# Seven block products for the first two up blocks of each MLP chunk, and quadrant moves on ScalarE

## The reference, cut to what matters

```python
for layer in range(2):
    h = rmsnorm(x, norm_mix_w[layer])
    x = x + (hybrid_mixer(h, ...) if layer == 0 else swa_sink_attention(h, ...))
    h = rmsnorm(x, norm_mlp_w[layer])
    u = relu(h @ w_up[layer])             # w_up 2048 x 8192
    x = x + (u * u) @ w_down[layer]       # w_down 8192 x 2048
return rmsnorm(x, final_norm_w)
```

## Time and profile before

| | |
|---|---|
| median of three runs | 1994.04 us |
| the profiled execution | 1995.09 us |
| its span, first to last instruction | 1993.3 us |
| mean granted TensorE clock | 0.999 |
| PE busy | 1984.1 us, 100% |
| DVE busy | 1581.1 us, 79% |
| ACT busy | 1066.0 us, 53% |
| matmuls | 9089 |

### The profile page before, as it was taken

How to read it: one execution, slowest core, us unless ns; L and a number is a source line. 1 busy time by engine, 2 the same in 40 slices (tenths; PEclk the granted TensorE clock), 3 DMA queues, 4 the chain that set the end, 5 groups by cost and what they waited for, 6 DMA issues and landing times.

```text
span 1993.3 us, 25055 instructions
## 1 busy us (share of the span) xinstructions
PE 1984.1 (100%) x9089; PEld 1638.8 (82%) x9089; DVE 1581.1 (79%) x2190; ACT 1066.0 (53%) x1402; POOL 45.1 (2%) x55
## 2 busy tenths in 40 slices
PE   9999999999999999999999999999999999999998
PEld 7888888888888888888888878888888888888887
DVE  6777678989769868976889887989858876985875
ACT  6665665555445545544545566555445544544554
POOL 1110110000000000000000000000000000000000
PEclk9999999999999999999999999999999999999999
DMA  8556545655665475556655545564575555466563
GB/s 306 177 182 205 181 165 203 202 172 192 217 199 170 168 249 182 184 206 190 211 190 186 174 154 165 182 197 152 197 247 191 188 206 189 148 218 226 187 205 112
DMA packets 191758, 382.50 MB, mean 192 GB/s; under 512 B 6328, under 2 KB 7616, under 8 KB 191552
## 3 DMA queue, kind: packets, MB, share of 16 engines
q1 hardware_dynamic: 190288, 377.51, 56.5%
q0 software_dynamic: 1216, 3.88, 0.6%
q10 hardware_dynamic: 176, 0.07, 0.0%
HBM read 379.34 MB, written 2.10 MB: 191 GB/s over the span
## 4 chain that ended last, share of the span: by engine, by line
PE 98%; DVE 1%; issue 0%; ACT 0%; DMA 0%; ACTq 0%
PE acc L1399 26%; PE acc L1400 26%; PE acc L1401 26%; PE bank L1399 3%; PE bank L1400 3%; PE bank L1401 3%; PE acc L1426 1%; PE acc L1425 1%; PE acc L1427 1%; DVE area L1219 1%; PE bank L1427 1%; PE bank L1425 1%; PE bank L1426 1%; PE bank L1515 0%; PE bank L1592 0%; PE bank L1616 0%
## 5 line engine op out<-in xcount | busy, mean ns | idle before, releaser
L976 DVE TENSOR_TENSOR w_lo<-raw,w_hi 128x1024 fp32r<-128x1024 f32 x744 | 899.8, 1223 | 354.4 <-ACT w_hi L733 350.1
L733 ACT ACTIVATE w_hi<-raw 128x1024 fp32r<-128x1024 f32 x744 | 777.2, 1059 | 716.7 <-PE acc L1401 562.4
L1399 PE MATMUL acc<-w_hi,a_hi 128*128 128x512 f32 x1552 | 607.1, 391 | 0.0
L1401 PE MATMUL acc<-w_hi,a_lo 128*128 128x512 f32 x1552 | 604.1, 389 | 0.0
L1400 PE MATMUL acc<-w_lo,a_hi 128*128 128x512 f32 x1552 | 604.0, 389 | 0.0
L1399 PEld LDWEIGHTS acc<-w_hi,a_hi 128*128 128x128 f32 x1552 | 291.5, 188 | 61.2 <-issue 0.9
L1401 PEld LDWEIGHTS acc<-w_hi,a_lo 128*128 128x128 f32 x1552 | 291.4, 188 | 60.8
L1400 PEld LDWEIGHTS acc<-w_lo,a_hi 128*128 128x128 f32 x1552 | 291.4, 188 | 59.9
L1399 PE MATMUL acc<-w_hi,b_hi 128*128 128x512 f32 x784 | 305.7, 390 | 0.0
L1400 PE MATMUL acc<-w_lo,b_hi 128*128 128x512 f32 x784 | 305.3, 389 | 0.0
L1401 PE MATMUL acc<-w_hi,b_lo 128*128 128x512 f32 x784 | 305.0, 389 | 0.0
(11 more groups left out here) (240 smaller groups left out, 1296.8 us busy)
## 6 DMA issues: line engine op xcount, KB each, us to landing
raw<-in_mlp_w_up SPq DMA_DIRECT2D x128, 1024.0 KB, 5.4
raw<-in_mlp_w_down SPq DMA_DIRECT2D x128, 1024.0 KB, 5.1
raw<-in_hyb_w_in SPq DMA_DIRECT2D x44, 1024.0 KB, 5.3
raw<-in_attn_w_qkv SPq DMA_DIRECT2D x20, 1024.0 KB, 5.1
raw<-in_hyb_w_out SPq DMA_DIRECT2D x16, 1024.0 KB, 5.2
raw<-in_attn_w_out SPq DMA_DIRECT2D x16, 1024.0 KB, 5.1
raw<-in_hyb_w_in SPq DMA_DIRECT2D x5, 512.0 KB, 9.6
out_y<-x SPq DMA_DIRECT2D x4, 512.0 KB, 3.0
```

The lines of the kernel that those rows point to most:

```text
L733: nc.scalar.activation(w_hi[:, ring(b, h)], raw[:, q, 2 * e:2 * e + 2, :], ACT.Copy).then_inc(hi_ready, 2 if what == ("R", HALVES - 1) else 1)
L976: nc.vector.tensor_tensor(w_lo[:, ring(b, h)], raw[:, q, 2 * e:2 * e + 2, :], w_hi[:, ring(b, h)].bitcast(F32), ALU.subtract).then_inc(lo_ ...
L1399: nc.tensor.matmul(a, xh, wh, start=first, stop=False, skip_group_check=joins)
L1401: ins = nc.tensor.matmul(a, xl, wh, start=False, stop=last, skip_group_check=joins)
```

## The change

- The up blocks 0 and 1 of every chunk (8 pairs, `UP0`, `UP1`) become pairs with seven block products. Their steps are those of the down pairs up to R3, then L6, L7, a slot border, R4 to R7. They are no longer woven.
- The partial results are copied to tiles of their own, `part_l` and `part_r` (`add_part`), and `sum_pair` adds the accumulators to them; ACT takes relu from there.
- The token sums for the up pairs are made once for each MLP (`add_up_tokens` on DVE, in the slot of res 2, step 6), and cast for each chunk (`up_tokens` on ACT, `up_tokens_rest` on DVE: in the slot of res 3, steps 1 and 2, and in the later chunks in the second down pair, steps 12 and 13).
- For all up blocks and the last residual block ahead of each MLP, ACT moves the result into a tile `shifted` by 16 activations of 32 partitions x 256 elements, the square included (`squares`, `move_res`), at steps of their own. DVE then needs four transposes of 128 partitions x 256 elements (`turn_shifted`).
- The last residual block's x additions stay on DVE, one step later. Its sums of squares, root and inverse go from steps 1 to 5 to steps 10 to 13 of the up pair, and TensorE waits for its low parts ahead of L6.

```diff
-QUADRANTS_PAIR = {6: 4, 7: 4, 8: 4, 9: 4}
+SQUARES_UP0 = {2: 3, 3: 3, 4: 3, 5: 4, 6: 3}
+SQUARES_UP1 = {4: 4, 5: 4, 6: 4, 7: 4}
+SQUARES_AT = {0: 4, 1: 6, 2: 6}
+SQUARES_PAIR = {3: 2, 4: 2, 5: 2, 6: 2, 7: 2, 8: 2, 9: 2, 10: 2}
+RES_AT = {2: 1, 3: 3, 4: 1, 5: 1, 6: 1, 7: 4, 8: 1, 9: 4}
+LAST_SUMS_AT = 10
...
+UP0 = {m + PERIOD * c for m in (MLP0, MLP1) for c in range(CHUNKS)}
+UP1 = {b + 1 for b in UP0}
...
+MIXED = [("P", 1), ("L", 2), ("P", 5), ("L", 3), ("P", 2), ("P", 6), ("P", 4), ("L", 4), ("P", 7),
+         ("L", 5), ("P", 3), ("R", 2), ("R", 3)]
+DOWN_STEPS = MIXED + [("R", 4), ("R", 5), ("R", 6), ("R", 7), (None, 0), ("L", 6), ("L", 7)]
+UP_STEPS = MIXED + [("L", 6), ("L", 7), (None, 0), ("R", 4), ("R", 5), ("R", 6), ("R", 7)]
...
+            def squares(slot, k):
...
+                for n in range(done, done + at[k]):
+                    a, f = divmod(n, QUADRANTS)
+                    ins = nc.scalar.activation(shifted[f * QUAD:(f + 1) * QUAD, a], src[a * QUAD:(a + 1) * QUAD, :, :, f, :],
+                                               ACT.Square)
...
+                        if b in UP0:
+                            ins = nc.vector.tensor_copy((part_l, part_r)[side][:, tt, :], accumulator(right, src))
...
+            def sum_pair(slot, b):
+
+                part = up_stage(b)
+                dve.wait_ge(part_added, slot.pairs(4, 4, pair_of(b)[0]))
+                for tt in range(TT):
+                    nc.vector.tensor_tensor(part[:, tt, :], part[:, tt, :], accumulator(b, tt),
+                                            ALU.add).then_inc(pair_summed, 1)
...
+            def add_up_tokens(slot):
+
+                whole = part_l.rearrange("p t n -> p (t n)").rearrange("p (k s) -> p k s", k=4)
+                dve.wait_ge(turned_out, slot.count(N_TURNED, -1, INIT_HALVES))
+                link(nc.vector.tensor_tensor(whole, a_hi[:, 0:4, :].bitcast(F32), a_lo[:, 0:4, :].bitcast(F32), ALU.add))
...
+                link(nc.vector.tensor_tensor(s1, a21, a22, ALU.add))
+                nc.vector.tensor_tensor(s3, a11, a21, ALU.subtract)
+                link(nc.vector.tensor_tensor(s2, s1, a11, ALU.subtract))
+                nc.vector.tensor_tensor(s4, a12, s2, ALU.subtract).then_inc(up_added, 1)
...
+            def turn_shifted(slot, k, kind):
...
+                dst = turn.rearrange("p m (k t a c) -> p t (m k) a c", k=2, t=TT, a=QUADRANTS)
+                for a in range(QUADRANTS):
+                    ins = nc.vector.transpose(dst[:, :, :, a, :], shifted[:, a])
+                ins.then_inc(turned, 2)
...
+                    if (b in FIRST_PAIRS and what == ("R", 6)) or (b in (MLP0, MLP1) and what == ("L", 6)):
                         pe.wait_ge(turned_out, slot.count(N_TURNED, 0, INIT_HALVES))
```

More of the change, by code:

```diff
@@ L91 @@
 DIRECT = {"xb", "kv", "aq"}
-BY_QUADRANT = {"up", "res"} | DIRECT
+BY_QUADRANT = {"res"} | DIRECT
+BY_VECTOR = BY_QUADRANT | {"up"}
 SPLIT = {"g", "up", "res"}
@@ L125, with pair_of, unit_free, side_block @@
 SUM_COUNT = {5: 1, 7: 2, 6: 3, 4: 4}
-LAST_TURNED_AT = STEP_OF["R", 6]
+def pair_of(b):
+    first = b if b in PAIRS0 else b - 1
+    steps, units = (UP_STEPS, UP_UNITS) if first in UP0 else (DOWN_STEPS, DOWN_UNITS)
+    return first, steps, steps.index((None, 0)), units
+def unit_free(b, n):
+    _, steps, _, units = pair_of(b)
+    if n < 2:
+        return STEP_OF["P", 4 if n == 0 else 3] + 1
+    side, g = units[n]
+    return steps.index((side, 2 * g + 1)) + 1
+def side_block(b, side):
+    first = pair_of(b)[0]
+    return first + (side == ("R" if first in UP0 else "L"))
+LEFT = {side_block(b, "L"): (b in DOWN0 and b not in FIRST_PAIRS) for b in PAIRS0}
 WOVEN = ({MIX_OUT0, QKV0, ATT_OUT0}
          | {m + COLS * n for m in (MLP0, MLP1) for n in range(2 * CHUNKS)}) - PAIRS0
-NSTEP = [PAIR_SPLIT if b in PAIRS0 else len(PAIR_STEPS) - PAIR_SPLIT if b in PAIRS1 else HALVES
+NSTEP = [pair_of(b)[2] if b in PAIRS0 else len(pair_of(b)[1]) - pair_of(b)[2] if b in PAIRS1 else HALVES
          for b in range(NBLK)]
 STEP0 = [sum(NSTEP[:b]) for b in range(NBLK + 1)]
+def banks_of_blocks():
+    out, last = [], 1
+    for b in range(NBLK):
+        if b not in LEFT and not (b in DOWN0 and b not in FIRST_PAIRS):
+            last = 1 - last
+        out.append(last)
+    return out
+ACC_OF = banks_of_blocks()
 def ring(b, k):
@@ L148, in pair_step, with counts @@
 def pair_step(b, k):
-    if b in PAIRS0:
-        return PAIR_STEPS[k]
-    if b in PAIRS1:
-        return PAIR_STEPS[PAIR_SPLIT + k]
-    return None
+    if b not in PAIRS0 | PAIRS1:
+        return None
+    _, steps, split, _ = pair_of(b)
+    return steps[k + (split if b in PAIRS1 else 0)]
+def counts(b, k):
+    return 2 if b in PAIRS0 and k == NSTEP[b] - 1 else 1
 def weight_at(b, k):
@@ L162, in weight_at @@
     side, h = what
-    first = b if b in PAIRS0 else b - 1
+    first, _, _, units = pair_of(b)
     if side == "P":
@@ L240 @@
 SUMS_AT = {1: 0, 2: 1, 4: 2, 5: 3}
+N_PAIR_SUMS = [TT * sum(p < b for p in UP0 | UP1) for b in range(NBLK + 1)]
 N_EVAC_ACT = total(BY_ACT, TT)
@@ L272, in pairs, with ups @@
     def pairs(self, per, n, b=None):
-        return self.plus(per * sum(p < (self.b if b is None else b) for p in PAIRS0) + n, 2 * per)
+        return self.plus(per * sum(p < (self.b if b is None else b) for p in PAIRS0) + n, 3 * per)
+    def ups(self, n):
+        return self.plus(sum(p < self.b for p in UP0) + n, 1)
     def chunks(self, per, n):
@@ L398, in build @@
         place["at"] = 0
+        shifted = take(QUADRANTS, TT * NB // QUADRANTS).rearrange("p a (t k c) -> p a t k c", t=TT, k=COLS)
+        s_sum = take(4, 2, P)
+        s_up = take(4, 2, P)
+        part_l = take(TT, NB)
+        part_r = take(TT, NB)
+        place["at"] = 0
         kk_t = take(KV, SEQ)
@@ L762, in leave @@
                 b = slot.b - 1
-                act.wait_ge(half_used, slot.halves(late(b)))
+                if b not in UP0 | UP1:
+                    act.wait_ge(half_used, slot.halves(late(b)))
                 if b > 0 and BLOCKS[b - 1][0] in DIRECT:
@@ L1194, in turn_quadrants @@
             def turn_quadrants(slot, k, kind, j):
-                at = {tick + late(slot.b - 1): n for tick, n in quadrants_at(kind, slot.b - 1).items()}
+                at = quadrants_at(kind, slot.b - 1)
                 if k not in at:
@@ L1401, in products @@
                         ins = nc.tensor.matmul(a, xl, wh, start=False, stop=last, skip_group_check=joins)
-                ins.then_inc(half_used, 2 if what == ("R", HALVES - 1) else 1)
+                ins.then_inc(half_used, counts(slot.b, k))
             def product(slot, k, p):
```

234 lines of the change are left out of this document (163 added, 71 removed).

## The result

The changed kernel takes 2024.55 us (median of 4 runs, 2020.5 to 2025.99) against 1993.93 us for the kernel before: ratio 1.0149, 95% interval 1.0131 to 1.0167. It is slower by 1.5%, and the time lies outside the forecast range. The profiled execution took 2020.5 us, with a span of 2018.7 and a mean granted clock of 0.997. It is the fastest of the four: the other three took 2024.43 to 2025.99 us, at 0.994 and 0.995.

The account below looks back on a forecast made before the run. PE, busy 1984.1 of 1993.3 us, was taken as the bound. Terms -8.2 + 5.2 + 2.2 + 3.5 + 0.6 = +3.3 us on the median of 1994.04 gave 1997.3 us, range 1990.0 to 2002.0.

Parts of the forecast that it names:

- The matmuls: PE, eight up pairs: 6 matmuls fewer each, 9041 in all, 1.03 us saved per pair, -8.2 us.
- Durations: Instruction prices: large transpose 0.45 us from start to start, like a small one; ACT's 32-partition square 0.32 from start to start.
- that rival: DVE's large transposes take four times as long, 5.4 us more in place 3 six times: 2040 us, chance 0.02.
- Place 1: Entries of both MLPs: added work in an unbroken DVE queue makes cuts late, +5.2 us second MLP, +2.2 first.
- late already: Second MLP's entry: third cut, for res 3's step 2, would end at 1280.5 while PE wants it at 1279.9.
- Place 2: First up pair of each MLP: L6 waits for the last residual block, 1.75 us late twice, +3.5 us.
- Place 3: Up 3 into the first down pair, six places: P4's cut has 0.13 us cover left, 0.1 late each, +0.6 us.
- the rival with the small moves at 0.40: ACT's small moves cost 0.40 us, 1.2 past place 3's cover six times, +6.6 us: 2003.9 us, chance 0.09.
- At nothing: Up pairs of chunks 1 to 3: no loss, P4's cut keeps its thin cover of 0.19 us in all six places.

Follow-up runs that it names:

- e15_turn_first_later: Changed kernel with up pairs only in chunks 1 to 3, last residual block moved by DVE, up blocks' transposes ahead of the weight cut: 1988.39 us, ratio 0.9974.
- e14_turn_first: Changed kernel with one edit: DVE transposes an up block ahead of the weight cut in the step of its last square, not behind it: 2002.55 us.
- e2_pairs_only: Changed kernel with up blocks' squares back as one 128x512 per half on ACT and their 16 small transposes on DVE, up pairs kept: 2048.96 us.
- e11_split: Changed kernel with moves of up 2 and up 3 back on DVE, those of up 0 and up 1 by ACT: 2039.14 us.
- e3_wide_up2: Changed kernel with up 2's square in 4 instructions on 128 partitions instead of 16 on 32, its quadrants not moved: 2001.25 us.

## Why the prediction was wrong

**The matmuls, right.** 9041 of them, and 42.50 us for an up pair against 42.49 for a down pair. e15_turn_first_later shows the six pairs' gain in the time: 1995.5 for the moves alone less 6 x 1.03 is 1989.3, measured 1988.4. DVE is 76 us less busy, where the sums had some 70 (180 less 112).

**Durations, half right.** Four large transposes take 1.42 us (1.8 forecast), so that rival is out; one takes 0.412 us against 0.436 for a small one. The Trainium skill (Vector Engine (DVE) Microarchitecture Reference, § 3.8 The reshape front-end and per-opcode configuration) puts a 32 x 32 array in front of each bank of 32 lanes, which sustains one element per cycle and lane. By that the large one takes as long as the small one, and the trace agrees. A square takes 0.415 alone, as forecast, but 0.425 from start to start and not 0.32: the row from which the 0.32 was taken stands among instructions on the same 128 partitions, and each square goes to another group of 32 than its neighbour (last section).

**Place 1, mechanism right, size short.** 3.0 and 6.0 us against 2.2 and 5.2, with DVE's remainders as releaser at L2 and P6. The 0.77 us at L4 in both entries was not foreseen; it is nearly the whole difference. The step ahead of the second MLP that would be "late already" is there as well: res 3's step 2 is 0.76 us late, 0.6 forecast. Its cut is the second of the three and not the third, and the inserted sums stand ahead of it.

**Place 2, mechanism right, one term short.** L6 waits 2.48 and 2.42 us against 1.75. From the cast to PE's start it takes 6.4 us where the sum had 6.67. The cover was wrong: without the wait PE would have been at L6 at 415.78 - 2.48 = 413.30, 3.9 us after the cast and not 4.92.

```profile
409.42 1.06 ACT L829 ACTIVATE w_hi<-raw 128x1024 fp32r<-128x1024 f32 x1 [0.65 <-DMA raw<-in_mlp_w_up]
...
411.65 1.42 DVE L1422 STREAM_TRANSPOSE turn<-area 128x256 f32<-128x256 f32 x4
...
415.78 0.50 PE L1615 MATMUL bank<-w_hi,a_hi 128*128 128x512 f32 x1 [2.21 <-DVE a_lo L1221]
```

**Place 3 is the step that failed: 0.6 us forecast, 18.7 measured.** It asked only whether the cut of P4 comes in time. What PE waits for is up 2's last low part, ahead of P1. By the forecast's own numbers that part would have been there in time: up 3's first matmul was at 472.87 - 21.76 = 451.11, the transposes' end by the sum at 468.75, 17.6 us later, and the measured 3.45 us from there (a cut, a weight sum, the low parts) give 21.1, 0.7 under 21.76. Measured it is 23.98. The 2.9 us between are two terms:

- The cast from which the sum starts was taken at its old time, 0.20 us after up 3's first matmul. It starts at 631.01, 1.84 us after it, because ACT still has up 1's squares to do. A queue that the change loads was entered at its time before the change.
- From up 1's transposes to ACT's third weight cast behind them 12.4 us pass, and 10.4 were forecast: 16 squares at 0.425 are 6.85 us with their transitions, not 5.17, and a cast alone between squares takes 1.08, not 0.95.

Against that stand 0.8 us by which the transposes were priced too high, twice 0.4. The price of a square enters twice, through up 1 and through up 2: at 0.32 us the two terms would fall by 1.6 and 1.7 us (an estimate from these rows), and 23.98 would be 20.7, in time. That is the rival with the small moves at 0.40, which had 0.09 and 6.6 us: its mechanism decided, counted once where it acts twice, and measured against the wrong wait.

**And the price alone does not decide.** e14_turn_first has it unchanged and no wait. The sum of place 3 took the order of DVE's queue (cut, then transposes) as given and did not see that ACT, its casts done, stands idle until the transposes behind that cut are through: 1.54 us here, 46.5 us over the 32 up blocks.

**At nothing, right.** Chunks 1 to 3 show no wait in an up pair, with the 0.19 us of cover at P4.

## What to carry to other kernels

When work is moved to an engine, walk its queue from the last moment at which it is known to be idle, not from the place where the new work ends. For a block that passes from one engine to another and back, give the consumer's transposes (or whatever the other engine waits for) the place ahead of bulk work that nobody waits for yet: the same instructions in that order were worth 22 us here. And look for every wait that a stationary operand has, not only for the weights' waits that bind today.

## What the runs showed of the hardware

**When neighbours overlap.** On ACT two squares on 128 partitions take 0.71 us together (the run with wide squares), 0.40 each and so 0.31 apart; on 32 partitions with the same 256 elements four take 1.70, and each starts only when the one before has ended. The Trainium skill (VectorE: DVE Perf Modes, § The TRN2 errata) gives one price for such an instruction, 224 cycles and one per element, by which I estimate 0.40 us here. The trace agrees for one alone (0.40 and 0.415); in a queue the runs show 0.31 and 0.425.

```profile
635.70 0.71 ACT L901 ACTIVATE area<-stage 128x256 f32<-128x256 f32 x2
```

It is not the number of partitions that decides. A block's first square reads and writes partitions 0 to 31, where the 128-partition cast ahead of it starts too, and it overlaps that cast by 0.09 us. The fifth reads from partition 32 on and starts 0.02 us after the cast's end:

```profile
619.02 1.04 ACT L829 ACTIVATE w_hi<-raw 128x1024 fp32r<-128x1024 f32 x1
619.97 1.68 ACT L899 ACTIVATE area<-area 32x256 f32<-32x256 f32 x4
621.67 1.06 ACT L829 ACTIVATE w_hi<-raw 128x1024 fp32r<-128x1024 f32 x1
622.75 1.70 ACT L899 ACTIVATE area<-area 32x256 f32<-32x256 f32 x4
```

So it is in the whole trace of the changed kernel: the 22 first squares that stand directly behind a cast overlap it by 0.09 to 0.10 us. Behind a cast all later squares of a block start 0.02 us after its end, behind a square both squares and casts 0.01 us after its end, and each of these starts at another partition than the instruction before it, in what it reads or in what it writes. (The first squares behind a relu wait for its result.) No rows read here have 32-partition neighbours that start at the same partition, so for those it is not shown. DVE's small transposes show the same in e2_pairs_only: the first of a block starts at 629.07, 0.08 us before the cut ahead of it ends, the fifth at 632.11, 0.02 us after its cut. On DVE four transposes of 128x256 take 1.42 us, four of 32x256 1.78.

**What a wait costs behind its end.** A wait of PE can cost more than its length. Behind the wait of 1.83 us at 478.15 seven matmuls start 0.427 us after the one before, nearly twice 0.227, and the granted clock from 480 to 500 is 0.94 on the mean: for these matmuls it is the lower of the two levels (1.2 GHz). Then the rows return to 0.227:

```profile
481.79 0.63 PE L1616 MATMUL bank<-w_lo,b_hi 128*128 128x512 f32 x1
482.21 0.54 PE L1617 MATMUL bank<-w_hi,b_lo 128*128 128x512 f32 x1
482.60 0.39 PE L1615 MATMUL bank<-w_hi,b_hi 128*128 128x512 f32 x1
```

The same wait in the second chunk had none of it (clock 1.00), and of the changed kernel's six first products two have it. In the run with the up pairs alone, where the first products wait 3.3 us, such matmuls follow in all six places; in e11_split, with the same 3.3 us, in five of six. So the length of the wait alone doesn't decide it, and what does in a single place stays open.

It bears on the times. The executions of the changed kernel at a granted clock of 0.994 and 0.995 are 3.9 to 5.5 us longer than the profiled one at 0.997, and the kernels without those waits (0.998 to 0.999 in e3_wide_up2 and e14_turn_first) came out 3 to 5 us below what I had expected of them from the medians. That fits more such matmuls in the executions that were not profiled, but it was not tried by itself.
